# Second FFN, rounds 4 to 10: the convolution's unit as seven half-token products

## The chip, the cores and the metric

One core of a Trainium2 chip runs the whole program; the cores' common memory holds inputs and outputs. The metric is the device time of one execution in microseconds (us). PE is the matrix engine, DVE the vector engine, ACT the scalar engine, POOL the general engine, SP the engine that here only issues DMAs.

## The reference, cut to what matters

Two transformer-like blocks on x of 512 tokens by 1024 features, float32. The change is in the up part of the second block's feed-forward layer:

```
h = rms_norm_2(x, ffn_norm_g) * (1 + scale_f) + shift_f
u, v = jnp.split(h @ w_up, 2, axis=-1)          # (512, 1024) @ (1024, 2 * 2816)
u = causal_depthwise_conv(u, conv_w, conv_b)    # 3 taps over the tokens, per channel
x = x + gate_f * ((jax.nn.silu(u) * v) @ w_down)
return rms_norm_2(x, final_norm_g)
```

The u half goes through the convolution, the v half is its gate.

## The kernel before

Everything is kept features by tokens: `h_hi` and `h_lo` are [128, 8, 512], the feature tile k in the middle. To get float32 precision from the rounded type each operand is two parts, high and low, and one k step of a matmul is three (`split_product`, lines 2281 to 2285): high weights by high input, high by low, low by high. An output tile of 128 channels (`tile`, from line 2287) is 8 k steps, 24 matmuls of 512 columns, accumulated in a PSUM bank.

Weights come in units of 256 columns, 1 MB, two tiles: `raw[0]` and `raw[1]` in turn. SP issues a unit when `lo_done` says that both tiles that were in its buffer are split (`unit`, line 716; in the up part the loop at lines 780 to 787). For each tile ACT writes the high part, `w_hi[s % 4]` (lines 917 and 1251), when the load is there and PE has finished tile s - 4; POOL subtracts it from raw into `w_lo[s % 4]` (`lo`, lines 814 to 821); PE waits for `lo_done`.

The up part of the second layer is tiles 156 to 199 (`S_UP2`, `S_DOWN2`), 11 rounds of four: two of u (banks 0 and 1), two of v (banks 2 and 3) by `s % 4`. The first round is done in token halves behind the norm; the other ten are a loop on PE (`ffn_pe`, from line 2600), a loop on ACT (`ffn_act`, from line 1233), one on DVE (`ffn_dve`, from line 1916) and one each on POOL and SP. Per u tile: ACT's first tap with bias into `ua` (line 1258), DVE's two other taps from PSUM (1936, 1939), ACT's silu (1262). Per v tile: DVE's product with `ua` (1930), ACT's high part `g_hi` (1265) and DVE's low part `g_lo` (1955), which the down part reads. Each engine runs its instructions in the order written, and a wait holds all behind it. `freed["dve"]` counts taps and products; PE waits on it before it writes a bank again. Loading the silu table is in ACT's loop (line 1242).

The residual x, `xT`, lies untouched from the norm until the down part adds to it. The down part follows as straight code, tiles 200 to 223.

## Time and profile before

| | us |
|---|---|
| median of 3 runs (1352.37 to 1357.09) | 1354.9 |
| profiled execution, span | 1350.1 |
| profiled execution, whole | not given apart from its span |
| PE busy | 1333.5 (99%) |
| DVE busy | 802.3 (59%) |
| ACT busy | 618.4 (46%) |
| POOL busy | 619.3 (46%) |

The span goes from the first to the last instruction of one profiled execution. The whole time of that same execution isn't in the page, so the median of the runs stands beside its span; what is between them, 4.8 us, is start and end. PE's busy time is of pipelined matmuls, so it says that PE has hardly a gap, and not how much work it does in that time. Line numbers are those of the kernel before.

### The profile page before, as it was taken

To read this page: it belongs to the slowest core of one execution; us is meant where nothing else is said; L and a number is where in the kernel's file an instruction comes from. 1 tells how busy PE (TensorE), PEld (TensorE's weight loads), DVE (VectorE), ACT (ScalarE), POOL (GpSimd) and SP (SyncE) were. 2 spreads that over 40 slices of the span, in tenths; PEclk is the share of its full clock that TensorE was granted. 3 is DMA by queue.
4 is the path that set the end of the run, shared out by engine and by line. 5 is a ranking of instruction groups with operands and counts; after the bars stand their busy time and mean duration, and the time that the engine had idled before them with its cause. 6 is when DMAs were issued, how large, how long until landed. Compare 5 with 4: busy or idle time off the path is not lost.

```text
span 1350.1 us, 21809 instructions
## 1 busy us (share of the span) xinstructions
PE 1333.5 (99%) x8014; PEld 1125.5 (83%) x8014; DVE 802.3 (59%) x1626; ACT 618.4 (46%) x1064; POOL 619.3 (46%) x334
## 2 busy tenths in 40 slices
PE   8999999999999999999999998999999999999998
PEld 7878888888998888888889976788998888888887
DVE  5898875456778676767897968714652323221222
ACT  7237566464354545453223535675453434432222
POOL 7545232126364444444544479623354444444441
PEclk9999999999999999999999999999999999999999
DMA  7931121115535444445663232122132222233221
...
DMA packets 188315, 146.22 MB, mean 108 GB/s; under 512 B 21561, under 2 KB 186659, under 8 KB 188240
## 3 DMA queue, kind: packets, MB, share of 16 engines
...
q8 instruction: 50, 0.82, 0.3%
...
q0 software_dynamic: 512, 0.25, 0.1%
q14 instruction: 25, 0.20, 0.0%
...
## 4 chain that ended last, share of the span: by engine, by line
PE 91%; POOL 4%; DVE 2%; issue 1%; ACT 1%; DMA 0%; DVEq 0%; POOLq 0%; ACTq 0%
PE ps L2283 27%; PE ps L2285 27%; PE ps L2284 27%; POOL w_lo L820 2%; PE ps L2477 2%; PE ps L2533 1%; PE ps L2562 1%; POOL hg L656 1%; PE ps L2762 1%; DVE qd L2077 1%; DVE hf L2085 1%; POOL kd_odd L652 0%; PE ps L2735 0%; PE ps L2367 0%; PE ps L2806 0%
## 5 line engine op out<-in xcount | busy, mean ns | idle before, releaser
L820 POOL TENSOR_TENSOR w_lo<-raw,w_hi 128x1024 fp32r<-128x1024 f32 (+2 forms) x224 | 518.5, 2318 | 666.5 <-ACT w_hi L920 401.6
L2283 PE MATMUL ps<-h_hi,w_hi 128*128 128x512 f32 (+1 forms) x1336 | 497.2, 372 | 0.0
L2284 PE MATMUL ps<-h_lo,w_hi 128*128 128x512 f32 (+1 forms) x1336 | 493.3, 369 | 0.0
L2285 PE MATMUL ps<-h_hi,w_lo 128*128 128x512 f32 (+1 forms) x1336 | 493.0, 369 | 0.0
L2283 PEld LDWEIGHTS ps<-h_hi,w_hi 128*128 128x128 f32 x1336 | 251.8, 188 | 46.0 <-issue 4.7
L2285 PEld LDWEIGHTS ps<-h_hi,w_lo 128*128 128x128 f32 x1336 | 251.8, 188 | 42.8
L2284 PEld LDWEIGHTS ps<-h_lo,w_hi 128*128 128x128 f32 x1336 | 251.9, 189 | 40.7
L920 ACT ACTIVATE w_hi<-raw 128x1024 fp32r<-128x1024 f32 (+2 forms) x136 | 133.5, 984 | 215.3 <-PE ps L2285 194.5
L1251 ACT ACTIVATE w_hi<-raw 128x1024 fp32r<-128x1024 f32 x88 | 93.3, 1060 | 211.8 <-PE ps L2285 211.8
L2283 PE MATMUL ps<-g_hi,w_hi 128*128 128x512 f32 (+1 forms) x394 | 144.9, 368 | 0.0
L2285 PE MATMUL ps<-g_hi,w_lo 128*128 128x512 f32 (+1 forms) x394 | 144.4, 366 | 0.0
L2284 PE MATMUL ps<-g_lo,w_hi 128*128 128x512 f32 (+1 forms) x394 | 144.3, 366 | 0.0
L1887 DVE SCALAR_TENSOR_TENSOR ps<-ada,cond,ps 128x128 f32<-128x128 f32 x336 | 119.6, 356 | 12.0
L2283 PEld LDWEIGHTS ps<-g_hi,w_hi 128*128 128x128 f32 x394 | 74.3, 189 | 12.2
L2284 PEld LDWEIGHTS ps<-g_lo,w_hi 128*128 128x128 f32 x394 | 74.3, 189 | 12.1
L2285 PEld LDWEIGHTS ps<-g_hi,w_lo 128*128 128x128 f32 x394 | 74.3, 189 | 12.0
L1936 DVE SCALAR_TENSOR_TENSOR sq<-ps,small,sq 128x511 f32<-128x511 f32 x44 | 33.0, 750 | 78.1 <-ACT sq L1258 74.8
L2208 DVE SCALAR_TENSOR_TENSOR xT<-ps,small,xT 128x256 f32<-128x256 f32 (+1 forms) x22 | 13.3, 604 | 106.1 <-PE ps L2285 106.1
L1655 DVE SCALAR_TENSOR_TENSOR ps<-z,small,ps 128x512 f32<-128x512 f32 x106 | 70.4, 754 | 0.0
L1930 DVE TENSOR_TENSOR hn<-ps,sq 128x512 f32<-128x512 f32 x22 | 15.2, 691 | 85.9 <-ACT sq L1262 85.9
L1122 ACT ACTIVATE sc<-sc,stat 128x128 f32<-128x128 f32 (+3 forms) x64 | 35.5, 557 | 26.7 <-DVE stat L1668 26.5
L1806 DVE COPY pT<-ps 128x128 f32<-128x128 f32 (+3 forms) x32 | 15.7, 490 | 48.1 <-PE ps L2533 27.0
...
## 6 DMA issues: line engine op xcount, KB each, us to landing
ada<-in_ada_w SPq DMA_DIRECT2D x48, 512.0 KB, 3.8
raw<-in_ffn_w_up SPq DMA_DIRECT2D x22, 1024.0 KB, 4.9
raw<-in_w_up SPq DMA_DIRECT2D x22, 1024.0 KB, 4.9
raw<-in_w_in SPq DMA_DIRECT2D x21, 1024.0 KB, 5.1
...
raw<-in_w_out SPq DMA_DIRECT2D x4, 1024.0 KB, 5.2
```

Of the source, the lines that this page charges most:

```text
L820: pool.tensor_tensor(w_lo[slot % 4][:, 0:nk, :], part[:, :, slot % 2 * P:(slot % 2 + 1) * P], w_hi[slot % 4][:, 0:nk, :].bitcast(F32), ALU ...
L920: act.activation(w_hi[s % 4][:, 0:nk, :], part[:, :, s % 2 * P:(s % 2 + 1) * P], ACT.Copy).then_inc(hi_done, 1)
L1122: act.activation(x, x, ACT.Exp, scale=-1.0, bias=stat[:, 2 * (j % 2) + g:2 * (j % 2) + g + 1], accum_out=stat[:, 4 + 2 * (j % 2) + g:5 + 2 ...
L1251: act.activation(w_hi[s % 4][:, :, :], part[:, :, s % 2 * P:(s % 2 + 1) * P], ACT.Copy).then_inc(hi_done, 1)
L1655: ins = dve.scalar_tensor_tensor(out=out, in0=src, scalar=w, in1=was, op0=ALU.mult, op1=ALU.add)
L1806: dve.tensor_copy(pT[:, m % 2, 1, 0:L2], ps[7][:, 0:L2]).then_inc(pw_copied, 1)
L1887: dve.scalar_tensor_tensor(out=acc, in0=src, scalar=c, in1=acc, op0=ALU.mult, op1=ALU.add).then_inc(ada_scaled, 1)
L1936: dve.scalar_tensor_tensor(out=u[:, t, 1:T], in0=src[:, 0:T - 1], scalar=col(wname, m + wide), in1=u[:, t, 1:T], op0=ALU.mult, op1=ALU.add ...
L2283: pe.matmul(out_ap, w, x, start=first, stop=False, **kw)
L2284: pe.matmul(out_ap, w, xl, start=False, stop=False, **kw)
L2285: return pe.matmul(out_ap, wl, x, start=False, stop=last, **kw)
L2477: ins = pe.matmul(ps[4 + g][:, 0:L], queries[i][g][part][:, t * P:(t + 1) * P], keys[b][g][:, 0:L], start=part == 0, stop=part == 1)
```

## The change

In rounds 4 to 10 (r = 3 to 9 in the code, `R0` and `R1`) the two u tiles of a round are computed together as a two-by-two block product. The weights of the unit are four blocks W(n, kh) of 128 channels (n) by 512 features (kh), `w_block`; the input is four blocks B(kh, th) of 512 features by 256 tokens (th). Seven products of 4 k steps and 256 columns, each step again three matmuls, replace the 48 matmuls of 512 columns:

- 1: W(0,0) by B11. 2: W(0,1) by B21. Their sum is the first tile's first token half.
- 5: S1 = W(1,0) + W(1,1) by T1 = B12 - B11. 6: S2 = S1 - W(0,0) by T2 = B22 - T1. 7: W(0,0) - W(1,0) by T3 = B22 - B12.
- 3: W(0,1) - S2 by B22. 4: W(1,1) by T4 = B21 - T2.

ACT copies product 1 to the bank of the second tile (`copy_one`); 6 is accumulated on it. `seed_c12` on DVE adds product 5 to that into the first tile's second half, on which 3 accumulates. After 7, `make_c22` adds product 5 again: the second tile's second half; 4 accumulates into its first half. Both tiles then lie as 512 columns across a bank border (`up_out`).

The four weight sums are DVE operations each round (`w_add`), in place in raw or in `hn`. The four token sums T1 to T4 are made once, in rounds 2 to 4, on DVE and for T3 on POOL, split in high and low parts, and lie in part where `xT` was; x is copied to DRAM (`x_kept`) before and read back after round 10. Splits of the products are of half size and use halves of `w_hi[0]`, `w_hi[1]`. The order of splits is a list, `SPLITS`. SP loads the gate's unit of the next round ahead of the convolution's. The gate's product goes to `g_prod`, which is `g_lo`'s place. PE's order in a round is 1, 5, a part of the gate's first tile, 6, 2, a part, 7, 3, the rest, 4, the gate's second tile. The loops of the second up part become straight code, and ACT loads the silu table once.

```diff
+R0, R1 = 3, FT // 2 - 1
+IN_ORDER = (1, 5, 6, 2, 7, 3, 4)
...
+SPLITS = list(range(S_UP2 + 4 * R0))
+SPLITS += [(R0, j) for j in IN_ORDER[:4]] + [up_tile(R0, 1, 0)]
+for _r in range(R0, R1):
+    SPLITS += [(_r, 7), (_r, 3), up_tile(_r, 1, 1), (_r, 4)]
+    if _r + 1 < R1:
+        SPLITS += [(_r + 1, 1), (_r + 1, 5), up_tile(_r + 1, 1, 0), (_r + 1, 6), (_r + 1, 2)]
+SPLITS += range(S_UP2 + 4 * R1, S_END)
+SPLIT_NO = {x: n + 1 for n, x in enumerate(SPLITS)}
...
+def tiles_done(s):
+
+    return s + 1 + ((0, 1, -1, 0)[s % 4] if block_rounds(s) else 0)
+
+
+def half_slot(r, j):
+    q = (7 * (r - R0) + IN_ORDER.index(j)) % 4
+    return q // 2, slice(q % 2 * 4, q % 2 * 4 + 4)
...
+        t_at = [(ada_at, ada_at + 4096), (x_at, x_at + 4096), (x_at + 8192, x_at + 12288),
+                (G0 + 4 * T * 2 * R1, G0 + 4 * T * (FT + 2 * R1))]
+        t_hi = [sb(f"t{n + 1}_hi", [P, 4, HALF], F32R, at=t_at[n][0])[:, :, :] for n in range(4)]
+        t_lo = [sb(f"t{n + 1}_lo", [P, 4, HALF], F32R, at=t_at[n][1])[:, :, :] for n in range(4)]
+        t_sum = [sb(f"t{n + 1}_sum", [P, 4, HALF], at=t_at[n][1])[:, :, :] for n in range(4)]
+        g_prod = sb("g_prod", [P, FT, T], at=G0 + 4 * FT * T)
+        w_sum = hn[:, 0, :].rearrange("p (k n) -> p k n", k=4)
+        five = [rstd[:, n * HALF:(n + 1) * HALF] for n in range(2)]
...
+        def w_of(r, j):
+
+            return {1: w_block(r, 0, 0), 2: w_block(r, 0, 1), 3: w_block(r, 0, 1), 4: w_block(r, 1, 1),
+                    5: w_sum, 6: w_block(r, 0, 0), 7: w_block(r, 1, 0)}[j]
+
+        one_at = psum[:, 4 * 512 + HALF:5 * 512]
+        c12_at = psum[:, 5 * 512:5 * 512 + HALF]
+        c21_at = psum[:, 6 * 512 + HALF:7 * 512]
+        c22_at = psum[:, 7 * 512:7 * 512 + HALF]
+        five_at = psum[:, 7 * 512 + HALF:8 * 512]
+        B11, B12, B21, B22 = [(slice(4 * kh, 4 * kh + 4), slice(th * HALF, th * HALF + HALF)) for kh in range(2) for th in range(2)]
+
+        def up_out(r, kind, t):
+
+            if kind == 0 and R0 <= r < R1:
+                at = (4 + 2 * t) * 512 + HALF
+                return psum[:, at:at + T]
+            return ps[BANK[up_tile(r, kind, t)]][:, :]
+
+        def after_product(eng, r, j):
+
+            if j in (3, 4):
+                eng.wait_ge(tile_done, tiles_done(up_tile(r, 0, 0 if j == 3 else 1)))
+            else:
+                eng.wait_ge(product_done, ONCE + 5 * (r - R0) + (1, 5, 6, 2, 7).index(j) + 1)
...
                 if n >= 2:
-                    sp.wait_ge(lo_done, 2 * n - 2)
+                    s = 2 * n - 4
+                    sp.wait_ge(lo_done, SPLIT_NO[(s - S_UP2) // 4, 4] if block_rounds(s) and s % 4 == 0 else splits(s + 1))
...
-            w = a["w_up_2"][0]
             u0 = S_UP2 // 2
-            with sp.Fori(0, FT // 2) as i:
-                for half in range(2):
-                    n = u0 + half
-                    sp.wait_ge(lo_done, i * 4 + (2 * n - 2))
-                    sp.dma_start(raw[n % 2][:, :].rearrange("p (k n) -> p k n", k=KD),
-                                 k_tiles(w, 0, KD, i * 256 + half * FFN)).then_inc(raw_in[n % 2], 16)
-            for n in range(S_DOWN2 // 2, S_END // 2):
+            for n in range(u0, u0 + 2):
+                unit(n)
+            sp.wait_ge(freed["dve"], FREED[S_OUT2 + KD - 1][1])
+            for half in range(2):
+                ks = slice(4 * half, 4 * half + 4)
+                sp.dma_start(x_kept[:, ks, :], xT[:, ks, :]).then_inc(x_saved, 16)
+            for n in range(u0 + 2, u0 + 2 * R0 + 2):
+                unit(n)
+            for r in range(R0, R1):
+                unit(u0 + 2 * r + 3)
+                unit(u0 + 2 * r + 2)
+            for n in range(u0 + 2 * R1 + 2, S_DOWN2 // 2 + 2):
+                unit(n)
+            after_product(sp, R1 - 1, 6)
+            after_product(sp, R1 - 1, 7)
+            for half in range(2):
+                ks = slice(4 * half, 4 * half + 4)
+                sp.dma_start(xT[:, ks, :], x_kept[:, ks, :]).then_inc(x_back, 16)
+            for n in range(S_DOWN2 // 2 + 2, S_END // 2):
                 unit(n)
             for t, half, who, count in STORES[:-1]:
...
+            def product_lo(r, j):
+                w, ks = half_slot(r, j)
+                pool.wait_ge(hi_done, SPLIT_NO[r, j])
+                pool.tensor_tensor(w_lo[w][:, ks, :], w_of(r, j), w_hi[w][:, ks, :].bitcast(F32), ALU.subtract).then_inc(lo_done, 1)
...
+                pool.tensor_tensor(out, h_hi[:, B22[0], B22[1]].bitcast(F32), h_hi[:, B12[0], B12[1]].bitcast(F32),
+                                   ALU.subtract).then_inc(t3_summed, 1)
+                pool.wait_ge(t3_summed, ONCE + 1)
+                pool.tensor_tensor(out, out, h_lo[:, B22[0], B22[1]].bitcast(F32), ALU.add).then_inc(t3_summed, 1)
+                pool.wait_ge(t3_summed, ONCE + 2)
+                pool.tensor_tensor(out, out, h_lo[:, B12[0], B12[1]].bitcast(F32), ALU.subtract).then_inc(t3_summed, 1)
...
-            ffn_act(S_UP2, 1)
+            act.activation(scratch[:, :], eps_t[:, :], ACT.Silu)
+
+            def product_hi(r, j):
+                u = up_tile(r, 0, 0) // 2
+                q = 7 * (r - R0) + IN_ORDER.index(j)
+                if q < 4:
+                    act.wait_ge(tile_done, tiles_done(up_tile(R0 - 1, 0, q // 2)))
+                else:
+                    after_product(act, R0 + (q - 4) // 7, IN_ORDER[(q - 4) % 7])
+                if j in (1, 2, 4):
+                    act.wait_ge(raw_in[u % 2], RAW_COUNT[u])
+                else:
+                    act.wait_ge(w_summed, ONCE + 4 * (r - R0) + {5: 1, 7: 2, 6: 3, 3: 4}[j])
+                w, ks = half_slot(r, j)
+                act.activation(w_hi[w][:, ks, :], w_of(r, j), ACT.Copy).then_inc(hi_done, 1)
...
+            def copy_one(r):
+
+                after_product(act, r, 1)
+                act.wait_ge(freed["dve"], FREED[up_tile(r - 1, 0, 1)][1])
+                act.activation(c21_at, one_at, ACT.Copy).then_inc(one_copied, 1)
+
+            def copy_five(r):
+                after_product(act, r, 5)
+                if r > R0 + 1:
+                    act.wait_ge(c22_made, ONCE + r - R0 - 1)
+                act.activation(five[r % 2], five_at, ACT.Copy).then_inc(five_copied, 1)
...
+            r = R0 - 1
+            product_hi(R0, 1)
+            first_tap(r, 0)
+            t_part_hi(1)
+            product_hi(R0, 5)
+            first_tap(r, 1)
+            product_hi(R0, 6)
+            silu(r, 0)
+            product_hi(R0, 2)
+            silu(r, 1)
+            t_part_hi(2)
+            hi(up_tile(R0, 1, 0))
+            g_high(r, 0)
+            for r in range(R0, R1):
+                g_high(r - 1, 1)
+                copy_one(r)
+                product_hi(r, 7)
+                copy_five(r)
+                product_hi(r, 3)
+                hi(up_tile(r, 1, 1))
+                product_hi(r, 4)
+                if r == R0:
+                    t_part_hi(3)
+                first_tap(r, 0)
+                if r + 1 < R1:
+                    product_hi(r + 1, 1)
+                    product_hi(r + 1, 5)
+                    hi(up_tile(r + 1, 1, 0))
+                    silu(r, 0)
+                    first_tap(r, 1)
+                    product_hi(r + 1, 6)
+                    product_hi(r + 1, 2)
+                    silu(r, 1)
+                else:
+                    silu(r, 0)
+                    hi(up_tile(R1, 0, 0))
+                    hi(up_tile(R1, 0, 1))
+                    first_tap(r, 1)
+                    hi(up_tile(R1, 1, 0))
+                    silu(r, 1)
+                g_high(r, 0)
...
+            def w_add(r, j):
+
+                u = up_tile(r, 0, 0) // 2
+                before = ONCE + 4 * (r - R0)
+                if j == 5:
+                    dve.wait_ge(raw_in[u % 2], RAW_COUNT[u])
+                    if r > R0:
+                        dve.wait_ge(lo_done, SPLIT_NO[r - 1, 5])
+                    ins = dve.tensor_tensor(w_of(r, 5), w_block(r, 1, 0), w_block(r, 1, 1), ALU.add)
+                elif j == 7:
+                    dve.wait_ge(w_summed, before + 1)
+                    ins = dve.tensor_tensor(w_of(r, 7), w_block(r, 0, 0), w_block(r, 1, 0), ALU.subtract)
+                elif j == 6:
+                    dve.wait_ge(w_summed, before + 2)
+                    dve.wait_ge(lo_done, SPLIT_NO[r, 1])
+                    ins = dve.tensor_tensor(w_of(r, 6), w_of(r, 5), w_block(r, 0, 0), ALU.subtract)
+                else:
+                    dve.wait_ge(w_summed, before + 3)
+                    dve.wait_ge(lo_done, SPLIT_NO[r, 2])
+                    ins = dve.tensor_tensor(w_of(r, 3), w_block(r, 0, 1), w_of(r, 6), ALU.subtract)
+                ins.then_inc(w_summed, 1)
...
+            def first_t_sum():
+                t_add(0, hi_of(B12), hi_of(B11), ALU.subtract)
+                t_add(0, t_sum[0], lo_of(B12), ALU.add)
+                t_add(0, t_sum[0], lo_of(B11), ALU.subtract, True)
+
+            def second_t_sum():
+                dve.wait_ge(x_saved, LANDED + 32)
+                dve.wait_ge(t_summed, ONCE + 1)
+                t_add(1, hi_of(B22), t_sum[0], ALU.subtract)
+                t_add(1, t_sum[1], lo_of(B22), ALU.add, True)
+
+            def fourth_t_sum():
+                dve.wait_ge(t_summed, ONCE + 2)
+                t_add(3, hi_of(B21), t_sum[1], ALU.subtract)
+                t_add(3, t_sum[3], lo_of(B21), ALU.add, True)
+
+            def seed_c12(r):
+                after_product(dve, r, 6)
+                dve.wait_ge(five_copied, ONCE + r - R0 + 1)
+                dve.tensor_tensor(c12_at, c21_at, five[r % 2], ALU.add).then_inc(c12_seeded, 1)
+
+            def make_c22(r):
+                after_product(dve, r, 7)
+                dve.tensor_tensor(c22_at, c21_at, five[r % 2], ALU.add).then_inc(c22_made, 1)
...
+            dve.wait_ge(half_lo, 3 * PIECES)
+            for r in range(R0 - 1):
+                taps2(r, 0)
+                taps2(r, 1)
+                if r == R0 - 2:
+                    first_t_sum()
+                    second_t_sum()
+                gated_up(r, 0)
+                gated_up(r, 1)
+                if r == R0 - 2:
+                    t_part_lo(0)
+                g_low(r, 0)
+                g_low(r, 1)
+            r = R0 - 1
+            fourth_t_sum()
+            taps2(r, 0)
+            w_add(R0, 5)
+            w_add(R0, 7)
+            t_part_lo(1)
+            taps2(r, 1)
+            w_add(R0, 6)
+            gated_up(r, 0)
+            for r in range(R0, R1):
+                if r == R0:
+                    t_part_lo(2)
+                gated_up(r - 1, 1)
+                w_add(r, 3)
+                g_low(r - 1, 0)
+                g_low(r - 1, 1)
+                seed_c12(r)
+                if r == R0:
+                    t_part_lo(3)
+                make_c22(r)
+                if r + 1 < R1:
+                    w_add(r + 1, 5)
+                taps2(r, 0)
+                if r + 1 < R1:
+                    w_add(r + 1, 7)
+                    w_add(r + 1, 6)
+                taps2(r, 1)
+                gated_up(r, 0)
...
-            ffn_pe(S_UP2, 2)
+            first_round(S_UP2, 2)
+            for s in range(S_UP2 + 4, S_UP2 + 4 * R0):
+                if s == S_UP2 + 4 * R0 - 1:
+                    pe.wait_ge(lo_done, splits(s))
+                    pe.matmul(ps[5][:, 0:HALF], w_hi[s % 4][:, 0, :], h_hi[:, 0, 0:HALF], start=True, stop=True)
+                    pe.matmul(ps[6][:, HALF:T], w_hi[s % 4][:, 0, :], h_hi[:, 0, 0:HALF], start=True, stop=True)
+                tile(s, h_hi, h_lo)
+
+            def product(r, j):
+
+                w, ks = half_slot(r, j)
+                out = {1: one_at, 2: one_at, 3: c12_at, 4: c21_at, 5: five_at, 6: c21_at, 7: c21_at}[j]
+                if j in (5, 6, 7, 4):
+                    t = {5: 0, 6: 1, 7: 2, 4: 3}[j]
+                    x, xl = t_hi[t], t_lo[t]
+                    if r == R0:
+                        pe.wait_ge(t_low, ONCE + t + 1)
+                else:
+                    b = {1: B11, 2: B21, 3: B22}[j]
+                    x, xl = h_hi[:, b[0], b[1]], h_lo[:, b[0], b[1]]
+                pe.wait_ge(lo_done, SPLIT_NO[r, j])
+                if j == 1:
+                    pe.wait_ge(freed["dve"], FREED[up_tile(r - 1, 0, 0)][1])
+                elif j == 5:
+                    pe.wait_ge(freed["dve"], FREED[up_tile(r - 1, 0, 1)][1])
+                elif j == 6:
+                    pe.wait_ge(one_copied, ONCE + r - R0 + 1)
+                elif j == 7:
+                    pe.wait_ge(c12_seeded, ONCE + r - R0 + 1)
+                elif j == 4:
+                    pe.wait_ge(c22_made, ONCE + r - R0 + 1)
+                for k in range(4):
+                    ins = split_product(out, w_hi[w][:, ks.start + k, :], w_lo[w][:, ks.start + k, :], x[:, k, :], xl[:, k, :],
+                                        j in (1, 5) and k == 0, k == 3, skip_group_check=True)
+                ins.then_inc(tile_done if j in (3, 4) else product_done, 1)
+
+            for r in range(R0, R1):
+                s = up_tile(r, 1, 0)
+                product(r, 1)
+                product(r, 5)
+                tile(s, h_hi, h_lo, part=(0, 2))
+                product(r, 6)
+                product(r, 2)
+                tile(s, h_hi, h_lo, part=(2, 5))
+                product(r, 7)
+                product(r, 3)
+                tile(s, h_hi, h_lo, part=(5, 8))
+                product(r, 4)
+                tile(s + 1, h_hi, h_lo)
```

## Rows read from the trace of the kernel before

**Rows 1.** The page, its first line and part 1.
```profile
span 1350.1 us, 21809 instructions
PE 1333.5 (99%) x8014; PEld 1125.5 (83%) x8014; DVE 802.3 (59%) x1626; ACT 618.4 (46%) x1064; POOL 619.3 (46%) x334
```
**Rows 2.** Windows, busy time by engine: rounds 4 to 10.
```profile
core 0: us, PE busy (x) PEld busy (x) DVE busy (x) ACT busy (x) POOL busy (x), PEclk, DMA share, GB/s
1045.76:1198.08 152.32, 152.32 (x674) 126.17 (x672) 44.23 (x56) 65.55 (x84) 67.29 (x28) 1.00 0.29 96
```
**Rows 3.** Timeline of PE: start, duration; ends of two runs of matmuls.
```profile
933.41 0.39 PE L2283 MATMUL ps<-mixed_hi,w_hi 128*128 128x512 f32 x1
...
954.94 0.39 PE L2285 MATMUL ps<-mixed_hi,w_lo 128*128 128x512 f32 x1
...
955.28 0.28 PE L2284 MATMUL ps<-mixed_lo,w_hi 128*128 128x256 f32 x1
...
965.12 0.28 PE L2285 MATMUL ps<-mixed_hi,w_lo 128*128 128x256 f32 x1
```
**Rows 4.** Groups by form, POOL: busy us, mean ns, idle before; the whole span.
```profile
L820 POOL TENSOR_TENSOR w_lo<-raw,w_hi 128x512 fp32r<-128x512 f32 x16 | 22.6, 1410 | 53.2 <-ACT w_hi L920 53.2
L664 POOL TENSOR_TENSOR hq<-hq,hgo 128x512 f32<-128x512 f32 x4 | 5.1, 1282 | 15.3 <-ACT hgo L925 15.2
```
**Rows 5.** Groups by form: the gate's product, two of ACT; g_lo's min/median/max.
```profile
L1930 DVE TENSOR_TENSOR hn<-ps,sq 128x512 f32<-128x512 f32 x16 | 11.1, 692 | 67.0 <-ACT sq L1262 67.0
...
L920 ACT ACTIVATE w_hi<-raw 128x512 fp32r<-128x512 f32 x16 | 10.1, 630 | 14.3 <-PE ps L2285 14.2
L956 ACT ACTIVATE ps<-ps,few 128x256 f32<-128x256 f32 x4 | 1.8, 448 | 12.0 <-PE ps L2344 7.2 <-PE ps L2339 4.8
...
L1955 DVE TENSOR_TENSOR g_lo<-hn,g_hi x18: 677/867/1341, 1048.7 to 1223.8; 128x512 f32 x18
```
**Rows 6.** Timeline: DVE and POOL together, two places.
```profile
957.04 2.48 DVE L1491 TENSOR_TENSOR rstd<-sq,rstd 128x512 f32<-128x512 f32 x1 [0.92 <-ACT sq L952]
956.57 2.41 POOL L820 TENSOR_TENSOR w_lo<-raw,w_hi 128x1024 fp32r<-128x1024 f32 x1 [3.04 <-ACT w_hi L920]
821.10 1.23 DVE L2085 TENSOR_TENSOR hf<-hf 128x1024 f32<-128x1024 f32 x1 [1.41 <-POOL hg L656]
822.36 3.27 DVE L2077 TENSOR_TENSOR qd<-hq,hf 128x1024 f32<-128x1024 f32 x1
821.14 3.40 POOL L820 TENSOR_TENSOR w_lo<-raw,w_hi 128x1024 fp32r<-128x1024 f32 x1
```
**Rows 7.** DMA issues: KB each, us to landing: up part's loads; two issued together.
```profile
raw<-in_w_up SPq DMA_DIRECT2D x6, 1024.0 KB, 4.9
...
317.95 0.37 SPq L720 DMA_DIRECT2D raw<-in_w_out  x1
318.36 0.58 SPq L730 DMA_DIRECT2D ada<-in_ada_w  x1
...
raw<-in_w_out SPq DMA_DIRECT2D x1, 1024.0 KB, 5.2
ada<-in_ada_w SPq DMA_DIRECT2D x1, 512.0 KB, 6.3
```
**Rows 8.** Timeline: hand-overs from ACT to POOL and between two taps.
```profile
1062.28 1.06 ACT L1251 ACTIVATE w_hi<-raw 128x1024 fp32r<-128x1024 f32 x1 [3.71 <-PE ps L2285]
1063.24 0.61 ACT L1262 ACTIVATE sq<-sq 128x512 f32<-128x512 f32 x1
...
1063.42 2.40 POOL L820 TENSOR_TENSOR w_lo<-raw,w_hi 128x1024 fp32r<-128x1024 f32 x1 [3.04 <-ACT w_hi L1251]
...
1097.69 0.75 DVE L1939 SCALAR_TENSOR_TENSOR sq<-ps,small,sq 128x510 f32<-128x510 f32 x1 [0.15 <-DVE sq L1936]
```
**Rows 9.** Round 2's last tap (timeline); the last 5 us (windows, columns as above).
```profile
1016.08 0.75 DVE L1939 SCALAR_TENSOR_TENSOR sq<-ps,small,sq 128x510 f32<-128x510 f32 x1
...
1345.00:1350.00 5.00, 0.44 (x5) 0.20 (x2) 1.42 (x3) 1.26 (x2) 0.00 (x0) 0.81 0.82 315
```

More of the change, by code:

```diff
@@ L1438, in _ @@
+            hi(up_tile(R1, 1, 1))
+            g_high(R1 - 1, 1)
+            for j in range(4):
+                hi(S_DOWN2 + j)
+                if j < 2:
+                    first_tap(R1, j)
+                else:
+                    silu(R1, j - 2)
+            for t in range(2):
+                g_high(R1, t)
             for n in range(20):
@@ L2868, in last_half @@
                 if half == 0:
[L2869 removed]
+                    pe.wait_ge(lo_done, splits(s))
                 else:
```

127 lines of the change are left out of this document (112 added, 15 removed).

## The prediction

> **What bounds the kernel now.** The page first [rows 1]: the PE is busy 99% of a 1350.1 us span and its clock is full in all slices. Then the stretches of the second feed-forward part [rows 2]: in the seven rounds that change (1045.76 to 1198.08) the PE has no idle time, DVE works 29%, ACT 43%, POOL 44%. Then the PE's order of time [rows 3]: from 933.41 to 954.94 lie 95 steps of a 512-column matmul, 226.6 ns each, and from 955.28 to 965.12 82 steps of a 256-column one, 120.0 ns. The busy time of one (0.39, 0.28) is pipelined and is not its price. A round is 96 matmuls x 226.67 = 21.76 us, as the windows have it. So columns bound the stage, and the other three engines have slack, on average. What decides is whether it lies where the new chains need it.
>
> The times below are of the profiled execution: span 1350.1. The page gives no total for it; the median of the runs, 1354.9, is 4.8 above, for start and end, which I leave as they are, so that a change of the span is added to 1354.9.
>
> **What the PE saves.** The convolution's unit was 48 matmuls x 226.67 = 10.88 us. It becomes 7 products x 12 matmuls x 120.0 = 10.08. The PE's own work falls by 0.80 per round, to 20.96; 7 rounds give -5.6, two extra 256-column matmuls +0.24: -5.4, or 1349.5. That is the most there is to gain, 0.4%; the products save 3072 of 24576 columns, 1.28 us at 2.4 columns a ns, and 36 more matmuls take 0.48 back, at the 13.3 ns that one costs beside its columns at either width (226.67 - 213.3, 120.0 - 106.7).
>
> **What it adds elsewhere, per round.** POOL: seven half splits for two whole ones, 7 x 1.3 - 2 x 2.4 = +4.3 us (1.28 is the price of a 128x512 of two SBUF inputs, 1.41 the mean of the half split [rows 4]). ACT: seven half splits at 0.63 for two at 1.06, two 256-column copies at 0.45 [rows 5, 8]: +3.2, less the table load that goes. DVE: four weight sums of 128x512 at 0.69 (between the fastest g_lo, 0.677, and the gate's product, 0.692 [rows 5]) and two 256-column sums at 0.42: +3.6. All fit in 21 us as sums. As chains they don't, for two reasons that the rows show.
>
> **The port.** A DVE operation with two SBUF inputs and a POOL operation shut each other out [rows 6]. At 957.04 a 128x512 add begins beside a split on POOL that runs to 958.98; it lasts 2.48 and ends 0.54 after the split. At 821.10 DVE has the port to 822.33; POOL's split, begun at 821.14, takes 3.40 for its 2.40 and ends at 824.54; DVE's next, begun at 822.36, lasts 3.27, to 825.63, 1.1 after POOL's end. Weight sums, g_low and the token sums are of this kind; taps, the gate's product and the two PSUM sums are not (they read PSUM; taps are 0.75 throughout [rows 8, 9]). The Trainium skill, "SBUF — State Buffer", section "SBUF: two separate sides", says that the pair of ports is an exclusive lock, held for the whole instruction, for a DVE operation with two SBUF inputs against a POOL one that reads SBUF. By that rule a round is the 25.9 below, by a fair sharing of bandwidth about 22; the trace agrees with the lock.
>
> **The two loads.** Before, a load is issued when its buffer's second tile is split, about every 10.9 us, and lands 4.9 later [rows 7]. After, the gate's load of the next round is issued behind the split of the gate's second tile, and the convolution's behind the split of product 4, next in POOL's order, 1.3 later. They queue: at 317.95 a 1 MB load was issued and landed in 5.2, one of 0.5 MB at 318.4 landed in 6.3, so about 1.5 after it [rows 7]: 3.0 us for 1 MB. The convolution's weights land 4.9 + 3.0 = 7.9 after the issue of the gate's.
>
> **The chain of one round.** Waits on raw for the next round's weight sum 5 stand in DVE's queue ahead of both tiles' taps, sums 7 and 6 ahead of the second tile's taps; product 5 of the next round waits for those taps (it writes a bank whose other half they read). Hand-overs between engines are 0.08 to 0.15 [rows 8]; I take 0.12. From the end of the second tile's taps, round r, to the same point of the next (durations [rows 4, 5, 8]; g_high has the size of a half split, 0.63):
> silu 0.61, gate's product 0.69, g_high 0.63, three hand-overs: 2.29. ACT's copy of product 1, split of product 7: 1.08. POOL waits for g_low on the port: 0.67. Splits 7 and 3 and of the gate's tile, 1.3 + 1.3 + 2.4 = 5.00 (ACT feeds them faster). Both loads 0.12 + 7.9 = 8.02. Weight sum 5: 0.81. First tile's taps 0.75 + 0.12 + 0.75 = 1.62. Sum 7: POOL meanwhile splits products 1 and 5, so it waits 1.04, then 0.69. Sum 6 needs sum 7; POOL's split of the gate's first tile has been waiting and takes the port: 2.40, then 0.69. Second tile's taps 1.62. Together 25.93 us, 4.97 more than the PE's 20.96.
> So the PE ends the gate's second tile, does product 1 and stands 4.9 us in one piece at product 5, each round. Nothing that the PE does is in this chain, so it costs nothing there if its clock falls meanwhile (in the last 5 us of the span, nearly idle, the mean is 0.81, against 1.00 before [rows 9]): products 3 and 4, whose results the taps read, end over 3 us before the taps are reached.
> Against 21.76 that is +4.2 for a round. The first link of the chain, round 4 to 5, still lives on the lead of the loads issued earlier: 25.4.
>
> **Into the block rounds.** In the two rounds before, port users pile up. From the taps of round 2 (they end at 1016.8 [rows 9]) until the split of the first gate tile is done: DVE 10 operations of 128x1024 at 1.23 (seven for token sums, three low parts), 3 weight sums and 2 g_low at 0.69, 15.8 us; POOL third_sum 3 x 2.40, two whole splits 4.8, four half splits 5.2, the gate's tile 2.40, 19.6. End to end 35.4, the operations of third_sum and DVE's taking the port in turn. With the waits in ACT's queue (silu, the second tile's first tap and high parts ahead of that split) I get 38.6, to 1055.6. The PE could be there at 1002.24 + 43.7 + 2.9 = 1048.8: it waits 6.8. With the 0.8 saved and 0.2 for hand-overs round 4 is 27.9 (+6.2). Without those queue waits it is 3.2 less, the low end of this term.
> Out of it: round 11 is plain; its first split is behind the late load: landed 2.6 before the PE is free, then 1.06 + 2.40 and hand-overs 0.4: +1.2.
> The extra 2 MB out and 2 MB back for x have no cost: out before round 2, where the next load is wanted 5 us later than it lands, back in round 11, and first read by the residual, behind four or more tiles of the down part, over 20 us by 226.7 ns a matmul. Loops that become straight code cost nothing: the tiles of the down part, straight code now, also step at 226.7. If x came late, each us would count on the path.
>
> **Sum.** +6.2 (round 4), +3.6 (round 5), 5 x 4.2 = +21.0 (rounds 6 to 10), +1.2 (round 11): +32.0, so 1354.9 + 32.0 = 1386.9; the two overlaps of ACT's successive operations (0.1 each [rows 8]) take off some 0.7 in round 4: **1386**. Bounds of the unknowns: half splits 1.28 to 1.41 and 2.8 to 3.3 us per 1 MB move a round by -0.4 to +0.8, -3 to +6 in all; round 4 by -3 to +2; a hand-over of 0.08 or 0.16 on the average gives -2 or +3. With lucky grants of the port (sum 6 before the gate's split, 2.4 less per round) it is 17 less, 1369. Own range 1369 to 1397.
>
> **Rivals.**
> - The port costs nothing in the chain (DVE slips between POOL's operations): 25.93 - 0.67 - 1.04 - 2.40 = 21.8, some 22.2 with ACT's first tap of tile 2, which then ends last. Rounds 4 to 6 use up the lead and keep 20.96, the rest give it back: 1353 to 1358, say 1355. For it: POOL is busy 44% only [rows 2]. Against it: both meetings in [rows 6], and that the weight sums fall where three of POOL's splits are released by the same load. 0.13.
> - Everything fits, the faster side: one mechanism, the convolution's load landing before 17 us into the round rather than at 23, so that sums and taps end before product 5. It needs the port rival and 1 to 2 us more, such as the loads not queueing (3.0 less: 18.8, below 20.96). Then 1349.5. For it: the mean load of 96 GB/s. Against it: the 6.3 us of the load behind another. 0.12.
> - Worse: the two queues turn each other's waits into a longer order (a g_low between splits 7 and 3 costs 0.7, a late hi of product 4 the load's issue 1 to 2): 28 per round, 1402. 0.07.
> - The forecast: 0.68.
>
> About 0.3% (4 us) is what a measurement tells from no change. Faster by more needs the second rival: 0.12. Same: the first, with a little of the others: 0.13. Slower: 0.75. The range that leaves two in ten out reaches down into the no-change case: 1353 to 1400.
>
> **What would show it.** In the profile after: 256-column steps of 120 ns; the PE idle some 5 us once per round before product 5, released by DVE's taps; DVE idle before weight sum 5 until a load has landed, then sums 7 and 6 at about 1.7 and 3.1 for 0.69; the convolution's load landing about 6.6 after its own issue; one wait of 7 us at the first gate tile; rounds of 25.9 against 21.76. It is wrong if the PE's share stays at 99%, if the weight sums take 0.69 beside POOL, or if the load lands 4.9 after its issue.

## The result and the profile after

The changed kernel takes 1381.7 us (median of 4 runs, 1380.1 to 1381.9) against 1354.8 for the kernel before on the same chip: ratio 1.0202 [1.0186, 1.0218], 2% slower. The forecast was 1386 and slower, 31.1 above the kernel before; measured are 26.9. First the head of its page, to be read against [rows 1].

```profile
span 1379.8 us, 21988 instructions
PE 1342.6 (97%) x8268; PEld 1143.5 (83%) x8268; DVE 876.7 (64%) x1679; ACT 624.2 (45%) x1097; POOL 670.1 (49%) x372
```

The span is 29.7 longer, the median 26.9. In this trace product 1 of round 4 starts at 1049.37, where the kernel before started that round at 1045.76. Most of the shift arises in code that the change doesn't touch, and it is the PE's clock there (windows, columns as in [rows 2]; first the kernel before, then the changed one):

```profile
842.00:932.00 90.00, 87.85 (x648) 72.25 (x647) 40.85 (x88) 57.59 (x141) 39.29 (x17) 1.00 0.17 48
842.00:932.00 90.00, 87.84 (x642) 71.97 (x635) 37.91 (x86) 57.66 (x140) 37.28 (x17) 0.96 0.17 48
```

The granted clock is 0.50 from 856.4 to 859.8 and again from 924.7 to 928.1, and matmul for matmul each of the two puts the changed kernel 1.5 to 1.6 us further behind: 3.1 of the 3.6; 0.3 arise at the program's start, and 0.2 are the two extra matmuls. The experiments' traces start round 4 between 1045.8 (no such stretch) and 1049.8 (two of them). So I count from product 1 of round 4 on.

Windows cut at each start of product 1 (columns as in [rows 2]): rounds 4 to 7.

```profile
1049.37:1076.28 26.91, 23.86 (x134) 21.37 (x133) 15.67 (x14) 13.09 (x21) 17.04 (x10) 0.87 0.25 79
1076.28:1098.88 22.60, 21.26 (x133) 19.05 (x132) 10.13 (x14) 9.19 (x16) 11.70 (x9) 1.00 0.29 94
1098.88:1125.96 27.08, 22.82 (x134) 20.41 (x134) 15.04 (x16) 11.57 (x20) 16.61 (x11) 0.94 0.24 78
1125.96:1150.88 24.92, 22.57 (x133) 20.44 (x132) 12.65 (x14) 10.51 (x17) 14.11 (x10) 0.93 0.27 85
```

With 25.72, 25.32 and 24.91 for rounds 8 to 10 that is 177.5 us for seven rounds that took 152.3 [rows 2]: +25.1. The shift of 3.6, round 11 (+0.1) and the part behind it (+0.8) make up the 29.7. The PE's waits (us in all, times, longest), from 990 to 1260:

```profile
PE ps L2648 <- DVE sq L2480: 15.8, 6, 4.3
PE ps L2648 <- POOL w_lo L917: 4.2, 2, 3.0
```

L2480 is the second tap, L917 the split of a gate tile. Six times, in rounds 5 to 10, the PE stands at product 5 for a tap, as forecast, though for 1.3 to 4.3 us and not for 4.9. The first matmuls of two such product 5s (timeline of PE, idle time and its releaser in brackets):

```profile
1129.89 0.55 PE L2648 MATMUL ps<-t_hi,w_hi 128*128 128x256 f32 x1 [2.35 <-DVE sq L2480]
...
1155.37 0.36 PE L2648 MATMUL ps<-t_hi,w_hi 128*128 128x256 f32 x1 [2.90 <-DVE sq L2480]
```

From the first product 5 that waits (1079.21) to the last (1205.84) five cycles pass, 25.33 each; 25.93 was forecast. One cycle, from tap to tap, on POOL and then on DVE:

```profile
1135.84 2.40 POOL L917 TENSOR_TENSOR w_lo<-raw,w_hi 128x1024 fp32r<-128x1024 f32 x1
1138.20 1.30 POOL L923 TENSOR_TENSOR w_lo<-raw,w_hi 128x512 fp32r<-128x512 f32 x1
1147.88 1.31 POOL L923 TENSOR_TENSOR w_lo<-raw,w_hi 128x512 fp32r<-128x512 f32 x1 [8.38 <-ACT w_hi L1569]
1149.14 1.30 POOL L923 TENSOR_TENSOR w_lo<-hn,w_hi 128x512 fp32r<-128x512 f32 x1
1150.40 2.83 POOL L917 TENSOR_TENSOR w_lo<-raw,w_hi 128x1024 fp32r<-128x1024 f32 x1
```

```profile
1147.11 0.69 DVE L2460 TENSOR_TENSOR hn<-raw 128x512 f32<-128x512 f32 x1 [6.00 <-DMA raw<-in_w_up]
1147.72 0.74 DVE L2477 SCALAR_TENSOR_TENSOR sq<-ps,small,sq 128x511 f32<-128x511 f32 x1
1148.50 0.75 DVE L2480 SCALAR_TENSOR_TENSOR sq<-ps,small,sq 128x510 f32<-128x510 f32 x1
1149.16 1.83 DVE L2463 TENSOR_TENSOR raw<-raw 128x512 f32<-128x512 f32 x1
1151.03 2.75 DVE L2467 TENSOR_TENSOR raw<-hn,raw 128x512 f32<-128x512 f32 x1
1153.70 0.74 DVE L2477 SCALAR_TENSOR_TENSOR sq<-ps,small,sq 128x511 f32<-128x511 f32 x1
1154.48 0.75 DVE L2480 SCALAR_TENSOR_TENSOR sq<-ps,small,sq 128x510 f32<-128x510 f32 x1
```

And the issue and landing of the convolution's load of that cycle:

```profile
L806 SPq DMA_DIRECT2D raw<-in_w_up x1: 367/367/367, 1139.5 to 1139.5; - x1
...
DMA to landing us min/median/max: 7.6/7.6/7.6
```

The gate's load is issued at 1138.27 behind the gate tile's split (1135.84 to 1138.24) and lands in 5.1, as one alone does [rows 7]; the convolution's, behind the next split (1138.20 to 1139.50), lands 7.6 after its issue, at 1147.1. Only then does DVE start sum 5 (L2460). Sum 7 (L2463) takes 1.83 for a 0.69 operation, since POOL's split from 1149.14 holds the port; sum 6 (L2467), behind another from 1150.40, ends 0.55 after that split's end, and the split itself took 2.83 for 2.40 behind sum 7. It is the pattern of [rows 6]. Over the stage:

```profile
L2467 DVE TENSOR_TENSOR raw<-hn,raw 128x512 f32<-128x512 f32 x7 | 17.2, 2459 | 0.2
L2463 DVE TENSOR_TENSOR raw<-raw 128x512 f32<-128x512 f32 x7 | 11.6, 1657 | 0.0
...
L2460 DVE TENSOR_TENSOR hn<-raw 128x512 f32<-128x512 f32 x6 | 4.2, 692 | 34.4 <-DMA raw<-in_w_up 34.4
```

Last, round 4's gate tile (timeline of PE):

```profile
1052.12 0.28 PE L2650 MATMUL ps<-t_hi,w_lo 128*128 128x256 f32 x1
1055.45 0.80 PE L2648 MATMUL ps<-h_hi,w_hi 128*128 128x512 f32 x1 [3.05 <-POOL w_lo L917]
1056.04 0.63 PE L2649 MATMUL ps<-h_lo,w_hi 128*128 128x512 f32 x1
1056.47 0.63 PE L2650 MATMUL ps<-h_hi,w_lo 128*128 128x512 f32 x1
...
1060.74 0.41 PE L2648 MATMUL ps<-h_hi,w_hi 128*128 128x256 f32 x1
...
1061.30 0.28 PE L2648 MATMUL ps<-h_hi,w_hi 128*128 128x256 f32 x1
1061.42 0.28 PE L2649 MATMUL ps<-h_lo,w_hi 128*128 128x256 f32 x1
```

It waits 3.2 us (1055.45 less 1052.12, less the 0.12 of a step). Behind the wait the steps are 0.43 at 512 columns and 0.21 at 256, where [rows 3] have 0.227 and 0.120: 512 columns in 0.427 are 1.2 a ns, the lower of the clock's two levels. It lasts until 1061.2 and costs 2.7 us: 1.4 on six wide steps, 1.3 on fifteen narrow ones. 21.04 + 3.2 + 2.7 make the 26.9 of the round.

### The profile page after: what moved, and what is told of

It is laid out like the page before. It is cut to its first block, busy times and chain, and to the rows that moved or that the text cites. A ratio compares the mean times of both kernels' runs of the same rounds, so it can differ in the third digit from the quotient of the medians.

```text
span 1379.8 us, 21988 instructions
## 1 busy us (share of the span) xinstructions
PE 1342.6 (97%) x8268; PEld 1143.5 (83%) x8268; DVE 876.7 (64%) x1679; ACT 624.2 (45%) x1097; POOL 670.1 (49%) x372
## 4 chain that ended last, share of the span: by engine, by line
PE 76%; DVE 8%; POOL 8%; DMA 4%; ACT 2%; issue 2%; SPq 0%; DVEq 0%; ACTq 0%; POOLq 0%
PE ps L2648 22%; PE ps L2649 22%; PE ps L2650 22%; DMA raw<-in_w_up 4%; POOL w_lo L917 4%; POOL w_lo L923 2%; PE ps L2842 2%; PE ps L2898 1%; PE ps L2927 1%; DVE raw L2467 1%; DVE t_sum L2496 1%; POOL hg L741 1%; DVE raw L2463 1%; DVE sq L2480 1%; DVE sq L2477 1%
## 5 line engine op out<-in xcount | busy, mean ns | idle before, releaser
L917 POOL TENSOR_TENSOR w_lo<-raw,w_hi 128x1024 fp32r<-128x1024 f32 (+2 forms) x210 | 491.1, 2344 | 569.2 <-ACT w_hi L1038 436.4
L2648 PE MATMUL ps<-h_hi,w_hi 128*128 128x512 f32 (+1 forms) x1308 | 481.2, 368 | 4.2 <-POOL w_lo L917 4.2
L2649 PE MATMUL ps<-h_lo,w_hi 128*128 128x512 f32 (+1 forms) x1308 | 476.5, 364 | 0.0
L2650 PE MATMUL ps<-h_hi,w_lo 128*128 128x512 f32 (+1 forms) x1308 | 475.3, 363 | 0.0
L2650 PEld LDWEIGHTS ps<-h_hi,w_lo 128*128 128x128 f32 x1308 | 248.7, 190 | 39.4
L1038 ACT ACTIVATE w_hi<-raw 128x1024 fp32r<-128x1024 f32 (+2 forms) x166 | 164.6, 994 | 249.6 <-PE ps L2650 218.0
L923 POOL TENSOR_TENSOR w_lo<-raw,w_hi 128x512 fp32r<-128x512 f32 x42 | 59.2, 1422 | 66.5 <-ACT w_hi L1569 66.3
L1369 ACT ACTIVATE w_hi<-raw 128x1024 fp32r<-128x1024 f32 x44 | 46.5, 1057 | 90.4 <-PE ps L2650 90.4
L2441 DVE SCALAR_TENSOR_TENSOR xT<-ps,small,xT 128x256 f32<-128x256 f32 (+1 forms) x22 | 13.3, 604 | 106.2 <-PE ps L2650 106.2
L1569 ACT ACTIVATE w_hi<-raw 128x512 fp32r<-128x512 f32 x42 | 25.6, 623 | 55.0 <-DMA raw<-in_w_up 23.7
L2648 PE MATMUL ps<-t_hi,w_hi 128*128 128x256 f32 x112 | 34.1, 304 | 15.8 <-DVE sq L2480 15.8
L1240 ACT ACTIVATE sc<-sc,stat 128x128 f32<-128x128 f32 (+3 forms) x64 | 35.5, 555 | 26.6 <-DVE stat L1901 26.5
```

The costliest lines, as they stand in the source:

```text
L917: pool.tensor_tensor(w_lo[slot % 4][:, 0:nk, :], part[:, :, slot % 2 * P:(slot % 2 + 1) * P], w_hi[slot % 4][:, 0:nk, :].bitcast(F32), ALU ...
L923: pool.tensor_tensor(w_lo[w][:, ks, :], w_of(r, j), w_hi[w][:, ks, :].bitcast(F32), ALU.subtract).then_inc(lo_done, 1)
L1038: act.activation(w_hi[s % 4][:, 0:nk, :], part[:, :, s % 2 * P:(s % 2 + 1) * P], ACT.Copy).then_inc(hi_done, 1)
L1240: act.activation(x, x, ACT.Exp, scale=-1.0, bias=stat[:, 2 * (j % 2) + g:2 * (j % 2) + g + 1], accum_out=stat[:, 4 + 2 * (j % 2) + g:5 + 2 ...
L1369: act.activation(w_hi[s % 4][:, :, :], part[:, :, s % 2 * P:(s % 2 + 1) * P], ACT.Copy).then_inc(hi_done, 1)
L1569: act.activation(w_hi[w][:, ks, :], w_of(r, j), ACT.Copy).then_inc(hi_done, 1)
```

## The experiments

**The two loads swapped.** Theory A, the forecast's: a chain of loads, port and taps sets the cycle. Its rivals: the port alone, or the PE's own work and its lower clock.

```diff
+                unit(u0 + 2 * r + 2)
                 unit(u0 + 2 * r + 3)
-                unit(u0 + 2 * r + 2)
```

> The changed kernel with one edit: in the block rounds SP issues the convolution's load of the next round ahead of the gate's. Theory A (the chain of one round runs through the two queued loads): the convolution's load is issued some 1.3 us later than the gate's was, behind the split of product 4, but lands 4.9 to 5.1 after its own issue and not behind 1 MB more, so weight sum 5 starts 1.7 to 2.4 us earlier in each of rounds 5 to 10 and the round goes from 25.3 to 23.1 (+-0.5): 1368 us, 1364 to 1373. Theory B (the wait at weight sum 5 is only where slack shows, and the port sets the round): within 3 us of 1381.7. Theory C (the PE's own work and its lower clock set the round): within 1 us.

Measured: 1366.9 us (2 runs), ratio 1.0098 [1.0074, 1.0123]; 15 us come back for a swap of two lines. Rounds 5 to 10 take 23.2 each on the mean, as theory A has it. The PE's waits:

```profile
PE ps L2648 <- DVE sq L2480: 9.0, 5, 2.3
PE ps L2648 <- POOL w_lo L917: 3.1, 1, 3.1
```

So the load's place in the queue is in the chain; it is not all of it. Sum 6 still takes 2.57 on the mean.

**Product 4's split ahead of the gate's second tile, with the swap.** The convolution's load is then issued one gate split, 2.4 us, earlier.

```diff
-    SPLITS += [(_r, 7), (_r, 3), up_tile(_r, 1, 1), (_r, 4)]
+    SPLITS += [(_r, 7), (_r, 3), (_r, 4), up_tile(_r, 1, 1)]
...
                 product_hi(r, 3)
+                product_hi(r, 4)
                 hi(up_tile(r, 1, 1))
-                product_hi(r, 4)
```

> The changed kernel with the loads swapped as in the first, and product 4's split set ahead of the split of the gate's second tile on ACT and on POOL. Theory A: the convolution's buffer is free 2.4 us earlier too, the chain is 25.3 - 2.4 - 2.4 or less, under the PE's own 20.96, so rounds 5 to 10 take 20.96 each with no idle PE: 6 x 20.96 against the 150.6 us that they take now, -24.8: 1357 us, 1354 to 1361; what is left over the kernel before is round 4 (26.9 us, 5.2 over a plain round) less the 0.8 saved in each of the six. Theory B (the port alone costs 4 us per round wherever the loads land): not below 1372. Theory C (256-column products cost the PE more than 120 ns a matmul when set between 512-column parts): rounds above 22, not below 1364.

Measured: 1354.6 us (10 runs), ratio 1.0012 [1.0000, 1.0025]. Round 4 takes 25.66, rounds 5 to 10 take 21.04 each, and one wait is left:

```profile
PE ps L2648 <- POOL w_lo L917: 3.1, 1, 3.1
```

The cycle's loss is gone, with every weight sum and its port meetings kept (sum 6 2.39 on the mean). Here a chain shorter than the PE's round costs nothing; at 21.04 the columns bound again.

**The same order without the swap.** It tells whether the split's place alone helps.

```diff
-    SPLITS += [(_r, 7), (_r, 3), up_tile(_r, 1, 1), (_r, 4)]
+    SPLITS += [(_r, 7), (_r, 3), (_r, 4), up_tile(_r, 1, 1)]
...
                 product_hi(r, 3)
+                product_hi(r, 4)
                 hi(up_tile(r, 1, 1))
-                product_hi(r, 4)
```

> The changed kernel with product 4's split ahead of that of the gate's second tile, but with the loads in their old order, the gate's first. Theory A (the chain runs through the later of two queued loads): the gate's load now waits for a split that ends 1.3 to 1.4 us later, and the convolution's still stands behind it, so each of rounds 5 to 10 is 1.3 longer than the changed kernel's 25.3: some 1390 us, 1386 to 1394. So one half of the pair that gave 27 us together loses 8 by itself. Theory E (the order of the splits was worth the half of the gain, the loads the other half): 1369.

Measured: 1391.8 us (2 runs), ratio 1.0278 [1.0253, 1.0302]: worse than the change itself. Rounds 5 to 10 take 27.1 on the mean, where 26.6 was expected.

```profile
PE ps L2648 <- DVE sq L2480: 23.7, 6, 4.2
PE ps L2648 <- POOL w_lo L917: 4.0, 2, 3.1
```

SP takes its waits in written order, so the convolution's load stays behind the gate's, whose split is now the last of four. The effects of the two edits don't add up: one alone costs 10 us, on top of the other it gains 12.

**The weight sums off the port.** The first operand of each of the four comes from an idle PSUM bank; the sums then hold other numbers, and the output is not the reference's. One of the four:

```diff
-                    ins = dve.tensor_tensor(w_of(r, 7), w_block(r, 0, 0), w_block(r, 1, 0), ALU.subtract)
+                    ins = dve.tensor_tensor(w_of(r, 7), idle_bank, w_block(r, 1, 0), ALU.subtract)
```

> The changed kernel with the first operand of each of the four weight sums read from a PSUM bank that is idle in the block rounds in place of SBUF: same count, size, order and waits, but no longer two SBUF inputs; the sums hold other numbers, so the output is not the reference's. Theory A (the port costs about 3.4 us of the chain: sum 7 behind POOL's splits 1 and 5, sum 6 behind the gate's split): sums take 0.69 each, rounds 22 to 23.2 in place of 25.3, 1366 us, 1361 to 1371, with the wait for the load still there. Theory B (DVE's longer sums are waits that overlap the load's): within 3 us of 1381.7.

Measured: 1365.0 us (2 runs), ratio 1.0084 [1.0064, 1.0105]. Sums 6 and 7, beside the same splits:

```profile
L2469 DVE TENSOR_TENSOR raw<-ps,raw 128x512 f32<-128x512 f32 x7 | 4.8, 690 | 0.2
L2465 DVE TENSOR_TENSOR raw<-ps,raw 128x512 f32<-128x512 f32 x7 | 4.8, 683 | 0.0
```

2459 and 1657 ns became 690 and 683. What makes them long is a second SBUF operand beside a split of POOL: sum 5 in the changed kernel, with two SBUF operands and POOL idle, takes 0.69 too. The Trainium skill, "SBUF — State Buffer", section "SBUF: two separate sides", says that a DVE operation with two SBUF inputs and a POOL one that reads SBUF lock each other out for whole instructions; these two pairs of means agree. The rest of the loss, with a load in the chain still, stays.

**More work for the PE where it stands.** Twelve matmuls of 256 columns ahead of product 5 in rounds 5 to 10.

```diff
+                    if r > R0:
+                        for _ in range(12):
+                            pe.matmul(ps[1][:, 0:HALF], h_hi[:, 0, 0:P], h_hi[:, 0, 0:HALF], start=True, stop=True)
```

> The changed kernel with 12 more 256-column matmuls on the PE in each of rounds 5 to 10, right before product 5 waits for DVE's taps, into an idle bank (the result is used by nothing). 1.44 us at 120 ns each, 6 times 8.6 in all. Theory A (the PE stands idle there for 1.5 to 4.5 us and is in no chain): 1381.7, within 2 us, the idle time before product 5 shorter by what was added, and less time at the lower clock behind it. Theory C (the lower clock behind the idle time sets the round): faster by 3 to 6, since the PE idles shorter. Theory D (the PE is the bound): +8.6, 1390.

Measured: 1382.4 us (4 runs), 0.7 above the change's 1381.7; ratio to before 1.0210 [1.0193, 1.0227].

```profile
PE ps L2648 <- DVE sq L2480: 10.4, 5, 2.8
PE ps L2648 <- POOL w_lo L917: 3.1, 1, 3.1
```

72 matmuls, 8.6 us at 0.120, for 0.7 us by the medians and 1.5 by the traces (rounds 4 to 10 in 178.9 for 177.5): 5.4 of them come out of the wait for the tap, and a part out of matmuls that ran at the lower clock. The PE is nearly off the path in this cycle, and so is what its clock costs it there.

**The third token sum earlier.** POOL makes it before the split of round 3's first u tile instead of before that of its first gate tile.

```diff
-                if x == up_tile(R0 - 1, 1, 0):
+                if x == up_tile(R0 - 1, 0, 0):
                     third_sum()
```

> The changed kernel with POOL's three operations for T3 one round half earlier, ahead of the split of the third round's first tile. The theory of the entry (POOL and DVE take the port in turn in rounds 2 and 3, the token sums late and with them all that is behind them): round 4 shorter by the 3.2 us that the PE waits at the gate's first tile and by the time at the lower clock behind that wait, 26.9 to 22 or 23; rounds 5 to 10 as they were: 1377, 1375 to 1379. Its rival (the three operations only fill POOL's slack, and ACT's queue alone makes the wait): round 4 stays at 26.9.

Measured: 1377.2 us (2 runs), ratio 1.0169 [1.0151, 1.0188]. Round 4 takes 21.95 and not 26.91; round 5 then takes 25.04 and not 22.60, as a PE that comes earlier stands longer at the chain. By the traces the seven rounds are 2.7 shorter (174.8 for 177.5), not the 5 of round 4 alone, so the expected rounds 5 to 10 "as they were" missed; the medians, 4.6 apart with two runs here, came out as expected.

**A PE kept busy through round 4's wait.** The second experiment with 26 matmuls that nobody uses where round 4 waits.

```diff
+                if r == R0:
+                    for _ in range(26):
+                        pe.matmul(ps[1][:, 0:HALF], h_hi[:, 0, 0:P], h_hi[:, 0, 0:HALF], start=True, stop=True)
```

> The second run's kernel with 26 more 256-column matmuls (3.1 us) on the PE in round 4, where it stands idle for 3.2 us in front of the gate's first tile; the result is used by nothing. If the idle time is what makes the six matmuls behind it take 2.7 us in place of 1.36 (the granted clock at its lower level): the matmuls behind it take 226.7 ns each, and round 4 is 24.3 in place of 25.7, the total 1.4 less. If the 3 us of idle time aren't the cause, round 4 stays at 25.7 or grows.

Measured: 1353.7 us (8 runs), ratio 1.0000 [0.9990, 1.0010]; the medians, 0.9 apart, don't settle a microsecond, but the timeline does (22 of the 26 have a record):

```profile
1050.75 2.80 PE L3265 MATMUL ps<-h_hi 128*128 128x256 f32 x22
1053.57 0.50 PE L2648 MATMUL ps<-h_hi,w_hi 128*128 128x512 f32 x1
1053.91 0.40 PE L2649 MATMUL ps<-h_lo,w_hi 128*128 128x512 f32 x1
```

Round 4 is 24.46 in place of 25.66, and the six wide matmuls behind the wait take 1.5 in place of 2.7. So beside the standing itself the wait cost what the clock took, here 1.2.

**All together.** The second experiment's two edits, the third token sum early, and the fourth token sum and T2's low part behind weight sum 6.

```diff
-            fourth_t_sum()
             taps2(r, 0)
             w_add(R0, 5)
             w_add(R0, 7)
-            t_part_lo(1)
             taps2(r, 1)
             w_add(R0, 6)
+            fourth_t_sum()
+            t_part_lo(1)
```

> The changed kernel with both edits of the second run, the early T3, and in round 3 the fourth token sum and T2's low part behind the second tile's taps and weight sum 6. Round 4 then has a wait of 1 us at most (it is 25.7 in the second run, 3.2 of wait and 1.4 at the lower clock), all block rounds 21.0: 7 x 21.04 + 0.2 + 1 against 7 x 21.76, 3.8 to 5 us below the kernel before: 1350, 1348.5 to 1352, ratio 0.9965. If the sum of the parts doesn't hold, round 4 keeps over 23 and it is 1352 or more.

Measured: 1352.1 us (11 runs), ratio 0.9988 [0.9976, 0.9999], short of the 0.9965 expected. In the trace, of an execution 4 us above that median (1356.05), round 4 is 21.65, as expected; round 5 is 24.68, which was not: the PE waits 2.1 for a tap and loses 1.6 to the lower clock. A part of it begins on DVE in round 4:

```profile
1049.51 0.68 DVE L2487 TENSOR_TENSOR g_prod<-ps,sq 128x512 f32<-128x512 f32 x1
1050.11 2.82 DVE L2504 TENSOR_TENSOR t_lo<-t_sum,t_hi 128x1024 fp32r<-128x1024 f32 x1
1052.86 0.68 DVE L2487 TENSOR_TENSOR g_prod<-ps,sq 128x512 f32<-128x512 f32 x1
```

The low part of T3 (L2504) waits for the port with the gate's second product behind it; behind that are g_high and product 7's high part, so POOL's next three splits begin at 1055.10 and the loads are issued from 1059.05. They also landed slowly, 7.5 and 6.8 us after issue, though nothing had been issued ahead of the first.

**That low part later.**

```diff
-                if r == R0:
-                    t_part_lo(2)
                 gated_up(r - 1, 1)
                 w_add(r, 3)
                 g_low(r - 1, 0)
                 g_low(r - 1, 1)
+                if r == R0:
+                    t_part_lo(2)
```

> As e7_all, but the low part of the third token sum is taken by DVE after the gate's product of round 3's second tile, weight sum 3 and both g_low, not ahead of them. In e7_all's trace that low part took 2.82 us beside POOL's split, and through the gate's product, g_high and product 7's high part behind it POOL's next three splits began at 1055.10 and the loads of round 5 at 1059.05; round 5 then waited 2.4 us and lost 1.2 more at the lower clock (24.68 against 21.04). Theory A (the load's issue is what is late): the splits begin 2 to 2.5 us earlier, both loads too, and round 5 is 21.0 to 21.6: 3 us less than e7_all, a ratio to the kernel before of 0.996 to 0.9975, 1349.5 us (1348 to 1351.5). Theory B (the two loads, landed 7.5 and 6.8 us after their issue there, were slow by themselves and the wait stays): round 5 still 23 to 24.7 and the ratio 0.998 to 1.000. Rival C: product 7 now waits for the low part of the third sum: a new wait in round 4, ratio 0.998 to 1.000.

Measured: 1349.9 us (7 runs, 1348.0 to 1352.1), ratio to before 0.9973 [0.9961, 0.9984]: 0.3% faster than the kernel before and some 32 us below the change as it was made. POOL's three splits and the stage's windows:

```profile
1050.17 3.41 POOL L923 TENSOR_TENSOR w_lo<-raw,w_hi 128x512 fp32r<-128x512 f32 x2 [0.60 <-ACT w_hi L1569]
1054.16 1.67 POOL L923 TENSOR_TENSOR w_lo<-raw,w_hi 128x512 fp32r<-128x512 f32 x1 [0.58 <-ACT w_hi L1569]
```

```profile
1047.56:1194.84 147.28, 147.28 (x926) 133.59 (x925) 87.59 (x98) 74.57 (x119) 100.64 (x61) 1.00 0.29 101
```

Seven rounds of 21.04 = 147.28, without a wait of the PE and at full clock, where before they took 152.3: -5.0, and the part behind round 11 gives 0.8 to 1.0 back in every changed kernel; the medians differ by 4.0 (1353.8 and 1349.9).

What this last move alone is worth isn't shown. Counted from product 1 of round 4, the convolution's load is issued at 8.3 for 9.2 in the trace before and lands at 13.3 for 16.7: 0.9 of the 3.4 come from the move, 2.5 from the load's own time, 5.0 here and 7.5 there. Why it took 7.5 is open, and with 5.0 there the wait of 2.1 would have been all but gone without the move (an estimate from these times). The two ratios, 0.9988 and 0.9973, have intervals that overlap.

## Why the prediction was right, by its steps

- **What the PE saves: right.** A block round without waits is 21.04, forecast 20.96; the 0.08 lies in the wide matmuls behind each change of width. The limit for the seven rounds, 5.6, measured 5.0, and was reached only with five moves in the order of the work.
- **The chain of a round: right, 25.33 for 25.93.** The cycle shown is 25.48 from tap to tap. From the end of the taps at 1129.75 to the gate's load at 1138.27 it is 8.5 for 9.0 (POOL's split 7 begins 2.94 after the taps for 3.37, since successive operations of ACT overlap by 0.1; its wait for g_low on the port is there, 0.6); from that load to sum 5 8.84 for 8.02; sum 5 and first taps 2.05 for 2.43; sum 7 1.87 for 1.73; sum 6 2.67 for 3.09; last taps 1.5 for 1.62. The term that was mis-sized most is the loads, 0.8 too short: the second megabyte landed 3.7 behind the first (1147.1 and 1143.4) where 3.0 was taken from a load of half the size. The hand-overs, at 0.12 each too long, and sum 6 made up for it, so that the sum is nearer than its parts by luck. The gap between two landings isn't one number either: 3.3 to 4.3 us here, where the second load is issued 1.25 to 1.4 behind the first, but 2.7 where it is issued 0.4 behind (first and third experiment) or 2.4 behind (second and last). Nothing here says why.
- **That the load and the port are both in it: shown**, by the first and the fourth experiment, each giving back 15 to 17 us of the 27, and by the second, in which the chain falls below the PE's round and nothing is left of the loss.
- **The clock costs nothing in the chain: right there, wrong in round 4.** The lower level came with four of the six waits at product 5 (granted 0.93 to 0.94 in rounds 6 to 9, 1.00 in rounds 5 and 10). Of the 4.3 us by which a cycle is longer than 21.04 the PE stood still in 2.9 (the 15.8 without the first wait's 1.3, over five) and ran slower in most of the rest; the fifth experiment fills a part of the stand and moves the total by 0.7. In round 4, where the PE goes on by itself, the slower matmuls cost 2.7, which the sum had not.
- **Round 4: +6.2 forecast, 26.91 - 21.76 = +5.2 measured,** from a wait of 3.2 for 6.8 and 2.7 of clock. The sum was nearly right because one term was too large and one missing. The wait itself is near the low end given, 3.6, but not by the path given for it, DVE and POOL end to end without waits in ACT's queue. From round 2's last tap (1020.02) to the end of the gate's split 35.4 us do pass, yet POOL stands idle 6.4, 1.7 and 0.9 of them for ACT, and ACT's queue is the last link: between weight sum 6 and the high part of the gate's tile lie five of its operations.

```profile
1048.01 0.68 DVE L2467 TENSOR_TENSOR raw<-hn,raw 128x512 f32<-128x512 f32 x1
1048.79 0.63 ACT L1569 ACTIVATE w_hi<-raw 128x512 fp32r<-128x512 f32 x1 [2.60 <-DVE raw L2467]
...
1051.84 1.04 ACT L1038 ACTIVATE w_hi<-raw 128x1024 fp32r<-128x1024 f32 x1
1052.95 2.44 POOL L917 TENSOR_TENSOR w_lo<-raw,w_hi 128x1024 fp32r<-128x1024 f32 x1 [0.90 <-ACT w_hi L1038]
```

The sixth experiment shows that the token sums on the port are in that path as well: with T3 earlier, 5.0 of round 4's 26.91 go. The prediction's own figures have a slip here: 1016.8 and 38.6 make 1055.4, not 1055.6, so its wait is 6.6.

- **Round 5: the term that was off most in the total.** 25.4 forecast, 22.6 measured: the lead that round 4 leaves was counted 2.8 us too small. Round 6 gives 1.2 of it back (27.08 for 25.9), and rounds 7 to 10 are 2.8 below their forecast in all (100.87 for 103.7).
- **Round 11 and x:** the rest, from the end of round 10 to the down part, is 21.9 for 21.76, and from the down part's start to the end 131.1 for 130.3; the 1.2 forecast for round 11 stands as a wait of its split at the end of round 10. No wait for x shows: from the down part's first matmul to the last of all 125.2 us pass before and after. The 0.8 lies behind that last matmul, between its start and the end of the span (5.0 before, 5.8 after, 5.8 to 6.0 in the experiments), where only the last output and its stores are left; why they take longer stays open.
- **The rivals.** "The port costs nothing" falls by L2463 and L2467. "Everything fits" needed the convolution's load before 17 us into the round. Here it lands 21 in (1147.1 in the round from 1125.96); in the second experiment, with the port's price kept, it lands 13.3 in (1084.8 in the round from 1071.48), and the rounds are 21.04. "The queues turn each other into 28 per round" is not this kernel; rounds of 27.5 came only in the third experiment, by another order of the splits.
